# Products of two constants on TensorE, ahead of two meetings and beside the scores of two attentions

## The reference, cut to what matters

```
def joint_dense_attention(q, k, v, kc, vc):          # GQA: 8 heads of 64, 2 key heads
    ...
        sc = jnp.einsum('bqkgd,bnkd->bkgqn', qi, kk, preferred_element_type=jnp.float32) * (d ** -0.5)
        p = jax.nn.softmax(sc, axis=-1)
        return jnp.einsum('bkgqn,bnkd->bqkgd', p.astype(vv.dtype), vv)

def joint_window_attention(q, k, v, kc, vc, sink):   # the last attention: 128 queries against 3 blocks and the context
    ...
        p = jax.nn.softmax(jnp.concatenate([s_ctx, s_loc, s_snk], axis=-1), axis=-1)
        return (jnp.einsum('bkgql,blkd->bqkgd', p[..., :l].astype(vc.dtype), vc)
                + jnp.einsum('bkgqm,bmkd->bqkgd', p[..., l:l + 3 * Q_BLOCK].astype(vi.dtype), vi))
```

## Time and profile before

| | us |
|---|---|
| median of 3 runs | 2671.86 |
| lowest and highest of them | 2668.15, 2676.63 |
| the profiled execution, its own time | 2663.76 |
| its span, first to last instruction | 2662.5 |
| mean granted clock of TensorE | 0.947 of full speed |
| TensorE busy (matmul) | 2424.5 |
| VectorE, ScalarE, GpSimd busy | 959.0, 556.4, 214.5 |

### The profile page before, as it was taken

One profiled execution on the slowest core, in us unless ns is written; L12 is line 12 of the kernel. 1 busy time (PEld: TensorE's weight loads), 2 busy tenths in 40 slices (PEclk: granted clock), 3 DMA queues, 4 the chain that ended last, 5 costly groups with the idle time before them and its releaser, 6 DMA issues. The chain is left out here.

```text
span 2662.5 us, 27625 instructions
## 1 busy us (share of the span) xinstructions
PE 2424.5 (91%) x10465; PEld 1161.7 (44%) x10465; DVE 959.0 (36%) x2103; ACT 556.4 (21%) x1286; POOL 214.5 (8%) x381
## 2 busy tenths in 40 slices
PE   5988999959999888899999998989998799999998
PEld 2534576533343333233333333656444444454453
DVE  2666454362121111111211114532566762342281
ACT  1245431100000000000000002210555551210360
POOL 1000342020101000010000002000000000000000
PEclk8998999969999899899999999999799999999899
DMA  9201497439999999998999899110000002021000
GB/s 349 70 32 64 152 323 280 190 119 386 416 416 418 415 417 417 411 398 349 414 402 405 356 417 348 52 63 32 1 1 1 0 1 103 32 95 64 32 1 32
DMA packets 161392, 563.98 MB, mean 212 GB/s; under 512 B 18485, under 2 KB 42478, under 8 KB 127330
## 3 DMA queue, kind: packets, MB, share of 16 engines
q1 hardware_dynamic: 143000, 517.54, 49.6%
q0 software_dynamic: 15360, 39.43, 4.0%
q10 hardware_dynamic: 2890, 5.13, 0.5%
HBM read 535.72 MB, written 26.35 MB: 211 GB/s over the span
## 5 line engine op out<-in xcount | busy, mean ns | idle before, releaser
L218 PE MATMUL ps<-mem,ring 128*128 128x512 f32 (+1 forms) x1056 | 422.1, 560 | 2.6 <-DVE mem L790 1.6
L1839 PE MATMUL ps<-ring,mem 128*32 128x512 f32 (+2 forms) x1680 | 390.3, 611 | 17.9 <-issue 17.9
L218 PE MATMUL ps<-ring,mem 128*128 128x512 f32 (+5 forms) x1136 | 386.1, 496 | 18.4 <-ACT ring L2606 8.5
L218 PEld LDWEIGHTS ps<-mem,ring 128*128 128x128 f32 x1056 | 201.5, 192 | 213.2 <-issue 204.5
L218 PEld LDWEIGHTS ps<-ring,mem 128*128 128x128 f32 x1136 | 197.8, 193 | 191.9 <-issue 158.4
L224 PE MATMUL ps<-mem 128*128 128x128 f32 (+2 forms) x1155 | 186.0, 294 | 56.7 <-PEq L2258 10.2
L1839 PEld LDWEIGHTS ps<-ring,mem 128*32 128x32 f32 (+2 forms) x1680 | 134.5, 136 | 234.0 <-issue 234.0
L1839 PE MATMUL ps<-mem 128*32 128x512 f32 (+2 forms) x752 | 203.8, 629 | 12.3 <-issue 12.3
L224 PEld LDWEIGHTS ps<-mem 128*128 128x128 f32 (+2 forms) x1155 | 135.8, 146 | 181.2 <-issue 114.7
L1904 PE MATMUL ps<-ring,mem 128*32 128x512 f32 (+2 forms) x736 | 173.8, 603 | 14.8 <-issue 14.8
L1904 PE MATMUL ps<-mem 128*32 128x512 f32 (+2 forms) x672 | 181.1, 610 | 4.4 <-issue 2.7
(11 more groups left out here) (385 smaller groups left out, 2409.8 us busy)
## 6 DMA issues: line engine op xcount, KB each, us to landing
ring<-in_w_up SPq DMA_DIRECT2D x75, 2048.0 KB, 22.6
mem<-in_w_up SPq DMA_DIRECT2D x37, 2048.0 KB, 23.2
ring<-in_w_down SPq DMA_DIRECT2D x33, 2048.0 KB, 24.1
mem<-in_w_down SPq DMA_DIRECT2D x31, 2048.0 KB, 24.0
ring<-in_w_up SPq DMA_DIRECT2D x28, 1024.0 KB, 16.6
ring<-in_w_ada SPq DMA_DIRECT2D x12, 2048.0 KB, 9.3
ring<-in_mod_w SPq DMA_DIRECT2D x8, 2048.0 KB, 14.3
ring<-in_cd_w_in SPq DMA_DIRECT2D x6, 2048.0 KB, 7.8
```

Of the source, the lines that this page charges most:

```text
L218: i = e.matmul(o, l, r, start=(start and n == 0), stop=(stop and n == len(pairs) - 1))
L1839: m = e.matmul(PS[n][c0:c0 + rows, :], XGT[:, u, k * 128 + c0:k * 128 + c0 + rows], wt[:, kk, n * 512:n * 512 + 512], start=False, stop=(k ...
```

## The change

A helper `idle_products` is new. It multiplies `ident` with all 256 columns of `cst0` into the first half of a bank, n times. It is issued at four places:

- seven products after the last transposes of layer 1, ahead of the meeting before GQA, in the next bank of the rotation. `next_bank` waits until the bank's last content has been copied out, and the last product marks it free again.
- one product in GQA ahead of each `score(x + 1)` for which the steps x - 1 and x have no sums, from x = 3 on. By the list of sums these are x = 3 to 8, 15 to 20, 27 to 32 and 39 to 44, 24 products. They go into `PS[6]`, and where a group's values have been summed there before, they wait until VectorE has taken them.
- seven products after the last transposes of layer 2, ahead of the meeting before the last attention.
- three products in the last attention ahead of `score(2)`, also into `PS[6]`.

Nothing reads what they write. Nothing is removed or moved.

```diff
+    def idle_products(e, o, n):
+
+        for _ in range(n):
+            i = e.matmul(o[:, 0:256], ident, cst0, start=True, stop=True)
         return i
...
         pe_twice_t(e, "kt", lambda i: GKV[:, i, 0:128], 2, range(6))
+        o = next_bank(e, "idle1")
+        idle_products(e, o, 7).then_inc(*empties("idle1"))
...
-    def pe_attention(e, A, PB, filler, rate):
+    def pe_attention(e, A, PB, filler, rate, idle={}):
...
         score(0)
         for x in range(len(units)):
+            if x + 1 in idle:
+                taken_by = sum(j == len(A.groups[g][2]) - 1 for y in range(x) for g, j, *_ in A.sums[y])
+                if taken_by:
+                    e.wait_ge(*taken_.at(taken_by))
+                idle_products(e, PS[6], idle[x + 1])
             if x + 1 < len(units):
                 score(x + 1)
...
-    pe_attention(nc.tensor, gqa, PB, pe_latent(nc.tensor, 0), 1)
+    idle = {x + 1: 1 for x in range(3, len(gqa.units) - 1) if not gqa.sums[x - 1] and not gqa.sums[x]}
+    pe_attention(nc.tensor, gqa, PB, pe_latent(nc.tensor, 0), 1, idle)
...
         pe_twice_t(e, "wkt", lambda i: PKV[:, i, 0:128], 2, range(6))
+        o = next_bank(e, "idle2")
+        idle_products(e, o, 7).then_inc(*empties("idle2"))
...
-    pe_attention(nc.tensor, win, PB, no_filler(), 1)
+    pe_attention(nc.tensor, win, PB, no_filler(), 1, {2: 3})
```

More of the change, by code:

```diff
@@ L218, in products @@
             i = e.matmul(o, l, r, start=(start and n == 0), stop=(stop and n == len(pairs) - 1))
+        return i
+    def idle_products(e, o, n):
+        for _ in range(n):
+            i = e.matmul(o[:, 0:256], ident, cst0, start=True, stop=True)
         return i
```

## The result

The median went from 2675.89 us (5 runs of the kernel before, 2668.15 to 2683.66) to 2659.69 us (5 runs, 2656.03 to 2662.56). The ratio is 0.9937 with a 95% interval of 0.9918 to 0.9956, some 17 us (the medians differ by 16.2), clear of the 0.3% that the prediction took as the least that a measurement can tell.

What follows compares the result with a forecast made beforehand. TensorE at half clock was taken to bound the last attention and stretches of GQA. GQA's terms sum to -5.5 us, with the last attention's -11.1 to -16.6, giving 2655 us on the median of 2671.86; range 2643 to 2668.

Steps and rivals of the forecast that it cites:

- signs of being wrong: A clock of 0.50 again between `score(2)` and the first sums, or GQA as long as its 175.1 us before.
- Rival 1: The clock falls again inside the last attention until the first sums, losing half of 11.7 us: 2661 us; chance 0.25.
- The price: One added product on TensorE at the full clock: 0.53 us, with bounds of 0.45 and 0.75 us.
- The meetings: Seven products ahead of each meeting delay the first scores by 0.4 us in GQA and 0.6 in the last attention.
- The start of GQA: First scores and latent product at the full clock: -2.2 us, with the meeting's delay -1.8 us.
- The first slow stretch of GQA: 1893.72 to 1917.24 at the full clock, with VectorE's share at 0.8: 17.8 us, -5.7 us (-4 to -9).
- The second: GQA, 1949.34 to 1962.20: -1.3 us from the clock, +1.0 for products before it, together -0.3 us.
- the -1.3 in that sum: GQA, 1949.34 to 1962.20: 11.5 us in place of 12.86 with the clock up.
- Where TensorE was full: Added products in GQA cost +2.0 us in 1962.20 to 1998.52 and +2.5 in 2005.68 to 2046.94.
- The last attention: Full clock up to the first sums gives -11.7 us (-9.8 to -13), with +0.6 for the meeting -11.1 us.
- So I take it to stay: The clock holds in the last attention after `score(2)`, with pauses of 0.5 us a unit and none as long as 1.37.
- VectorE's pace: Last attention after `score(2)`: nine intervals, five of 2.49 and four of 2.03 us, 20.6 us in all.

Runs made afterwards that it cites:

- e1: The change without the 24 products in GQA and the three ahead of `score(2)`, only the seven at each meeting; ratio 0.9977 to the kernel before.
- e3: The change without its part in the last attention, neither the seven products ahead of that meeting nor the three; ratio 0.9960 to the kernel before.
- e4: The change plus one product ahead of each score from the fourth to the eleventh of the last attention, eight in all; ratio 0.9941 to the kernel before.
- e8: The change with 15 selected products in GQA and four more selected in the last attention; median 2643.55 us, ratio 0.9880 to the kernel before.
- e5: The change with 30 transposes in place of the seven products ahead of the last attention's meeting; one run, GQA 166.82 us, last attention 96.70 us.
- e6: The change plus two products ahead of each score from the fourth to the eleventh of the last attention; one run, GQA 166.81, last attention 93.04 us.
- e7: The change with 15 products at selected places in GQA in place of the 24, last attention as in the change; ratio 0.9915 to the kernel before.
- e2: The change without the 24 products in GQA, both meetings and the three products in the last attention kept; ratio 0.9966 to the kernel before.

## Why the prediction was right, and where it was not

The predicted time was 2655 us on a median of 2671.86, a ratio of 0.9937; the measured ratio is 0.9937, and the time of 2659.69 lies in the range. By steps it is less exact. The gain in the last attention was put at nearly twice what it is, and the timed runs show some 5 us of gain that the profiles do not place, which makes up for it. Of the prediction's own signs of being wrong one did appear, a clock of 0.50 between `score(2)` and the first sums. Rival 1, which came true in the last attention, had 2661 us, a ratio of 0.9959, just outside the measured interval.

1. **The mechanism.** Products in the pauses and ahead of the meeting hold the clock, and the stretches shorten with it: shown by the change and by e1, e3, e4 and e8, each of which moved the clock where it moved products, and the length of the stretch with it. That the pauses are what drops it is argued from what stands ahead of the falls, and the two pauses of 1.58 us with different ends (e3) show that they are not all of it. For the whole time the intervals are clear of the change's in e1 and e8 only. In the pauses nothing but products of 128 rows was tried, so it is not shown whether filling the pause or the kind of work counts.
2. **The price** was 0.53 us and is 0.456 (14 instructions in 3.19 us), near the lower bound.
3. **The meetings** were put at +1.0 us and cost nothing. From the first transpose to the first score it is 7.97 and 6.94 us, before 7.99 and 6.96. At the lower price the products end some 0.5 us ahead of ScalarE's last copy.
4. **The start of GQA**: from the first to the third score 7.64 us in place of 9.92, -2.3 against the -2.2 taken ahead of the delay.
5. **The first slow stretch of GQA**: -7.6 against -5.7. VectorE's share rose to 0.89 and not to the 0.8 taken; the bounds held it.
6. **The second**, 1949.34 to 1962.20: +2.4 for the same work and +2.8 with the units of the three products ahead of it, against -0.3. The step that failed is that the clock would stay up here, which the -1.3 in that sum supposes. One product ahead of the score that waits left 1.58 us of the 2.13, and the clock fell there in four profiles of the five with this program (the change, e4, e5, e6) and not in e3. After the fall two added products took 1.06 us each and not 0.60. Four products left 0.40 us, and the clock held both times (e7, e8).
7. **Where TensorE was full** the products cost 2.2 us in 1962.20 to 1994.50 and 1.7 in the last stretch; I had 2.0 and 2.5. One more, ahead of the second slow stretch, cost 0.4. Between the two, 1994.50 to 2005.68 gave 1.3 us, against 2.5, for there too the clock fell again. The parts of GQA are then -2.3 - 7.6 + 0.4 + 2.8 + 2.2 - 1.3 + 1.7 = -4.1 us.
8. **The last attention**: -6.0 against -11.1. The step that failed is "So I take it to stay". It was rival 1, to which I gave 0.25: from the third score on the clock stays for three scores (e5) or six (the change, e2, e7) and then falls. I had judged by the longest single pause, 1.37 us, and by a row of GQA. Here the clock fell after pauses of 0.3 to 1.1 us in four of six units, none as long as 1.37. VectorE's pace itself was right: the third to the eighth score took 11.47 us, 2.29 each, where 20.6 / 9 is 2.29.

Over the profiles the sum is GQA -5.6 (168.6 against 174.2) and the last attention -5.9 (94.9 in the change, e2 and e7, against 100.7 in before and e3), -11.5 together, where I had -16.6. The timed ratio says -17, with an interval from -12 to -22. That the time met the forecast is then partly luck. Where the rest lies stays open: GQA and its meeting alone are worth 10.7 us in the timed runs (e3), but the interval there, 4.0 to 17.1, has room for the 5.6 of the profiles. The falls differ from execution to execution, in GQA and also in the stage between, which took 455.9 to 463.0 us with no edit in it, and one profile of each kernel does not weigh them.

## What to carry to other kernels

Look at the granted clock beside the busy share. A TensorE that is busy for all of a stretch at 0.50, beside a vector engine with two thirds of that in work, is a candidate for products of constants. Put them into the pauses and leave them out where the engine is full: in GQA 15 placed so gave 160.00 us in two profiles, 24 spread by a rule 164.3 to 174.2. Do not judge by the longest pause: in the last attention 1.1 us and less went before a fall, and in GQA 1.32 and 1.46 us were passed without one. Where the next engine is the bound, four products in eight units (e8) kept the clock as eight did (e4) and made the stretch a microsecond shorter.

## What the runs showed of the hardware

- The same instructions can keep the clock in one execution and lose it in the next: GQA with the same 24 products took 164.32, 166.8 (twice), 171.01 and 174.18 us. A pause of 1.58 us ahead of the same score was passed at 1.00 in one of the five.
- Float32 transposes held the clock at 1.00 for 6.5 us as products did (e5), and sixteen of them were all that stood ahead of a rise from 0.50 to 0.99. Scores of 64 rows with transposes did not bring it back in 29 us of a full TensorE (e1). After the last product they went on at the full clock for some 7 us (e5) to 15 us (the change).
- After a fall ahead of the first sums of the last attention the clock came back only once products of values stood among the scores, in all seven profiles with such a fall, and in e1 and e3 the stage was 1.8 us longer than before with a later return.
